# Modulation stores half a part later in SyncE's queue, output written tile by tile, and constant products ahead of the turns

## The chip, the cores and the metric

The kernel runs on one core of a Trainium2 chip. Its engines work side by side, each through a queue of its own in order: TensorE (PE) multiplies, VectorE (DVE) and ScalarE (ACT) do elementwise work, GpSimd (POOL) computes small roots and starts the gathers, and SyncE (SP) starts transfers. An engine whose next instruction waits on a semaphore holds everything that is queued behind it. The metric is the device time of one execution in microseconds (us); less is better.

## The reference

Two networks are computed one after the other on the same x (256 tokens of 1024), all in f32. The first is two layers of a hybrid mixer (retention and a state-space scan) and a SwiGLU. The second is two layers with modulated norms, latent attention with a context of 256 tokens, Fourier and pooling branches, and an expert layer that gathers 128 rows of 2 x 1024 numbers for each token. The parts that the change touches:

```python
def _modulation(cvec, w_mod, b_mod):
    m = jax.nn.silu(cvec) @ w_mod + b_mod          # 1024 -> 6 x 1024, for c and for c_ctx, in each of 2 layers
    return jnp.split(m[:, None, :], 6, axis=-1)

def _modulate(x, g, shift, scale):
    return _rmsnorm(x, g) * (1 + scale) + shift

def _rmsnorm(x, g):
    xf = x.astype(jnp.float32)
    y = xf * lax.rsqrt(jnp.mean(xf * xf, axis=-1, keepdims=True) + EPS)
    return (y * g.astype(jnp.float32)).astype(x.dtype)
...
# the last steps: x + m5 * peer(modulate(x, ...)), then the final norm, which is the output
```

## The kernel before

**How it is laid out.** A class `Plan` writes one list of work items by hand (`put(kind, ...)`). Each engine's program then goes through that list once and issues what it has to do for each kind, so every engine's order is the list's order. Two streams are merged into the list by paces: the x stream (first network, then the second network on x) and the context stream (the modulation rows, then the context's first layer). The 256 tokens are two tiles (`tt`) of 128 rows. PSUM is used as eight banks that are handed out in rings (`take()`); `u.full` and `u.free` are the semaphores of a bank.

**The modulation** (`modulation`, lines 571 and after) runs in the context stream beside the first network's first layer. It has six parts (2 layers of 3), each 2048 columns wide, each summed over k = 0 to 7. For each k, GpSimd loads one 1 MB piece of `wmod` (`mod_weights`, L2202), and TensorE multiplies it (`mod`, L1281). After k = 7 VectorE adds the bias with four small instructions (`mod_add`, L1702), and SyncE stores the rows to DRAM (`mod_store`, L2254, four transfers that begin with a wait for that add). The rows are read back later by `mod_load` (L2264) and `load_row` (L2272).

**The weights of the first network** are loaded by the same SyncE queue (`weights`, L2227), 1 MB for each chunk of 256 columns, from a ring of three buffers: a load waits until TensorE is done with the chunk three before it. Three such loads are therefore the most that stand ready. A chunk is 16 products of 128x128 by 128x256 (L1089, two rows of the trace for each product).

**The norms ahead of turns.** In `norm_to_hT` and `modulate` ScalarE sums squares (L1968), VectorE scales the sum (L1499), GpSimd takes the root (L2196), the rows are scaled, and TensorE turns them by transposes (L1124, `row_turn` and `mod_turn`). `low_rank` has the same chain between a product and its turn. TensorE waits meanwhile.

**The expert layer** (`peer_x`) gathers 256 pieces of 1 MB (L2209). Buffers: 11 in layer 0, and 15 in layer 1, where four more come from the side arena (`spare`). For each piece VectorE forms a dot product (L1902), and after every four TensorE adds the second halves up (L1445). `add(tt)` (L1921, L1925) adds the tile's sum to X: tile 0 at step 140 of 256, tile 1 at the end.

**The end.** After both tiles are added, `final` loads the norm's gain row (L2288), sums the squares of both tiles (L1968), takes the root, scales both (L1682) and stores the whole output, 1 MB, with one transfer (L2290).

## Time and profile before

| | us |
|---|---|
| median of three runs | 4399.33 (4393.66 to 4401.11) |
| the profiled execution, its own time | 4395.78 |
| its span, first to last instruction | 4394.5 |
| TensorE busy | 3679.7 (84% of the span) |
| VectorE busy | 2364.5 (54%) |
| ScalarE busy | 599.5 (14%) |
| GpSimd busy | 1311.6 (30%) |
| mean granted TensorE clock | 0.921 of full speed |

Busy shares are means over stages with different limits. The timeline of SyncE's queue and of TensorE shows what each stage waits for; the views of waits add those up. In a view of windows, PEclk is the granted TensorE clock as a share of 2.4 GHz (0.50 is the lower level, 1.2 GHz), and the DMA share is the busy share of the 16 DMA engines.

### The profile page before, as it was taken

Reading aid. Unit: us, or ns where it says so; the run is one execution under the profiler, and the core shown is the slowest. Engines: PE = TensorE matmul, PEld = TensorE weight load, DVE = VectorE, ACT = ScalarE, POOL = GpSimd, SP = SyncE. Lnnn points to the kernel's source line nnn. Section 1 sums busy time; section 2 is a strip of 40 time slices with the busy share of each in tenths; the row PEclk is TensorE's granted clock in tenths of the full one; section 3 lists DMA queues with packets and bytes.
Section 4 is the critical chain, followed back from the end, with each engine's and each line's share of the span. In section 5 each row is a group of like instructions: output and inputs, shape, how many; then the busy total and the mean of one; then the engine's idle time right before and its main releaser. Section 6 shows DMA issues by size and latency. Waiting matters only on the chain. (4 is left out here: it accounts for less than half of the span.)

```text
span 4394.5 us, 40482 instructions
## 1 busy us (share of the span) xinstructions
PE 3679.7 (84%) x14400; PEld 2592.9 (59%) x14400; DVE 2364.5 (54%) x5571; ACT 599.5 (14%) x1567; POOL 1311.6 (30%) x1123
## 2 busy tenths in 40 slices
PE   7777899998898778999996898778776898877777
PEld 5555778887765667887854776333333687333332
DVE  3332111258667777767652114776774212877774
ACT  1112200110001111010001201111111221111111
POOL 1000000000574435766530002444442001444442
PEclk9888999999898888999997999988988999999999
DMA  8542233433898768999982246998997234999997
GB/s 309 211 178 109 96 145 148 158 125 125 324 407 338 258 228 304 399 408 380 381 319 88 96 147 270 421 410 335 419 421 306 104 115 184 396 421 421 421 421 312
DMA packets 209527, 1214.89 MB, mean 276 GB/s; under 512 B 23872, under 2 KB 25024, under 8 KB 97712
## 3 DMA queue, kind: packets, MB, share of 16 engines
q0 software_dynamic: 154368, 855.71, 48.8%
q1 hardware_dynamic: 54960, 356.60, 21.5%
q8 instruction: 117, 1.92, 0.2%
q14 instruction: 82, 0.67, 0.0%
HBM read 1211.07 MB, written 1.15 MB: 276 GB/s over the span
## 5 line engine op out<-in xcount | busy, mean ns | idle before, releaser
L1089 PE MATMUL bank<-big 128*128 128x256 f32 (+3 forms) x9848 | 2179.4, 382 | 142.5 <-DMA big<-in_w 78.6
L1089 PEld LDWEIGHTS bank<-big 128*128 128x128 f32 x9848 | 1857.8, 194 | 466.3 <-issue 148.0
L2209 POOL DMA_INDIRECT big<-in_pboth,big x1024 | 1246.6, 1217 | 1259.4 <-PE bank L1445 622.8
L1445 PE MATMUL bank<-big 128*128 128x512 f32 x2048 | 1000.5, 647 | 282.5 <-ACT big L2170 282.5
L1902 DVE CUSTOM_DVE_ANT_0 big<-big 128x1024 f32<-128x1024 f32 x768 | 923.1, 1223 | 308.5 <-DMA big<-in_pboth,big 300.2
L1445 PEld LDWEIGHTS bank<-big 128*128 128x128 f32 x2048 | 414.0, 207 | 866.1 <-issue 494.7
L2196 POOL TENSOR_TENSOR big<-big 128x2 f32<-128x2 f32 (+1 forms) x47 | 39.1, 835 | 1617.7 <-DVE big L1499 1617.3
L1913 DVE SCALAR_TENSOR_TENSOR big<-big 128x1024 f32<-128x1024 f32 x254 | 326.1, 1284 | 27.9 <-DMA big<-in_pboth,big 4.4
L1124 PE MATMUL bank<-big 128*128 128x128 f32 x572 | 105.7, 326 | 193.4 <-ACT big L1982 72.0
L1124 PEld LDWEIGHTS bank<-big 128*128 128x128 f32 x572 | 80.0, 170 | 217.3 <-issue 188.3
L2170 ACT ACTIVATE big<-big 128x128 f32<-128x128 f32 x512 | 164.3, 391 | 250.6 <-DVE big L1881 246.5
L1267 PE MATMUL bank<-big 128*128 128x512 f32 x352 | 152.1, 593 | 3.3 <-DVE big L1668 3.3
L1572 DVE SCALAR_TENSOR_TENSOR big<-big,bank 128x512 f32<-128x512 f32 x32 | 22.0, 687 | 209.3 <-ACT big L2008 198.9
L1556 DVE SCALAR_TENSOR_TENSOR big<-bank,big 128x255 f32<-128x255 f32 (+1 forms) x144 | 62.7, 477 | 129.8 <-ACT big L1996 128.1
L2160 ACT ACTIVATE big<-big 128x4 f32<-128x4 f32 x128 | 26.5, 207 | 767.8 <-DVE big L1877 767.8
L1267 PEld LDWEIGHTS bank<-big 128*128 128x128 f32 x352 | 66.4, 189 | 88.1 <-issue 83.3
L1758 DVE TENSOR_REDUCE big<-bank 128x1 f32<-128x512 f32 (+1 forms) x48 | 28.9, 603 | 161.5 <-PE bank L1346 160.6
L1780 DVE SCALAR_TENSOR_TENSOR big<-big,bank 128x512 f32<-128x512 f32 x36 | 24.8, 689 | 147.4 <-PE bank L1089 147.4
L1654 DVE SCALAR_TENSOR_TENSOR big<-big,bank 128x256 f32<-128x256 f32 x32 | 13.4, 420 | 138.9 <-PE bank L1089 128.5
L2202 POOL DMA_DIRECT2D big<-in_wmod x48 | 25.8, 542 | 198.7 <-PE bank L1281 198.7
L1968 ACT ACTIVATE big<-big 128x1024 f32<-128x1024 f32 x26 | 27.2, 1048 | 423.7 <-DVE big L1675 154.8
L1499 DVE TENSOR_SCALAR big<-big 128x2 f32<-128x2 f32 (+1 forms) x47 | 7.2, 161 | 123.2 <-ACT big L1968 116.9
(192 smaller groups left out, 2060.8 us busy)
## 6 DMA issues: line engine op xcount, KB each, us to landing
big<-in_w SPq DMA_DIRECT2D x104, 1024.0 KB
big<-in_wmod POOLq DMA_DIRECT2D x48, 1024.0 KB, 7.2
big<-in_wgu SPq DMA_DIRECT2D x44, 1024.0 KB
big<-in_wzg SPq DMA_DIRECT2D x36, 1024.0 KB, 4.8
big<-in_wro SPq DMA_DIRECT2D x32, 1024.0 KB
big<-in_wpq SPq DMA_DIRECT2D x24, 1024.0 KB, 4.8
big<-in_wd SPq DMA_DIRECT2D x22, 1024.0 KB
big<-in_pboth,big POOLq DMA_INDIRECT x1024, 14.9
```

The source lines that it names most:

```text
L1089: last = pe.matmul(o, a, b, start=(i == 0), stop=(i == n - 1))
L1124: last = pe.transpose(o[:, i, :], b, ident)
L1267: last = pe.matmul(u.ap, act[:, kk, tt * P:tt * P + P], wk[:, k, 512 * n:512 * n + 512], start=(kk == 0), stop=(kk == 21))
L1445: last = pe.matmul(u.ap, d.ap, row[:, 512 * i:512 * i + 512], start=(k == 0), stop=(k == 127))
L1556: i = v.scalar_tensor_tensor(c[:, m, s:256], o[:, m, 0:256 - s], conv["w"][m][:, 3 - s:4 - s], c[:, m, s:256], ALU.mult, ALU.add)
L1758: step(v.reduce_max(sm[:, c:c + 1], u.ap[:, 0:nk * P], AX.X))
L1902: v.tensor_tensor_reduce(row, row, h, 1.0, 0.0, ALU.mult, ALU.add, out).then_inc(done[0], 1)
L1913: v.scalar_tensor_tensor(at, s.ap, by, at, ALU.mult, ALU.add).then_inc(done[0], 1)
L1968: last = s.activation(dumps[tt], srcs[tt], ACT.Square, accum_out=r.sm[:, r.at + tt:r.at + tt + 1])
L2170: s.activation(d.ap, p.ident, ACT.Copy, scale=by).then_inc(diag[0], 1)
L2196: g.tensor_tensor(r.sm[:, 8 + r.at:8 + r.at + r.n], r.sm[:, 4 + r.at:4 + r.at + r.n], r.sm[:, 12:13].to_broadcast([P, r.n]), ALU.pow).then ...
L2209: g.indirect_dma_start(out=s.ap, out_offset=None, in_=table, in_offset=bass.IndirectOffsetOnAxis(ap=index, axis=0)).then_inc(s.full[0], 16)
```

## The change

Three things are changed.

1. **Stores.** `mod_store` of a part is kept back in a list (`late`) and put into the order just before the item `mod` with k = 3 of the next part. The last part's store stays where it was, after the loop.
2. **Output.** The final norm becomes one for each tile. Tile 0's statistics follow its `add(0)` at step 140, its scaling and its store (0.5 MB) are put at step 168; tile 1's follow `add(1)`. The gain row is loaded with the last mod row, at the start of the gather. It and a scratch row take the place of one of the four spare gather buffers (15 become 14). SyncE waits for both stores in a last item `finished`.
3. **Constant products.** TensorE gets products of the identity with a constant 128x256 tile, written into the bank that the turn is about to fill and then overwritten by it: 8 ahead of the wait for the root and 2 behind it in the four `norm_to_hT`; 12 and 7 in the four modulated norms of x; 8 ahead of the first turn in the four `low_rank` of x. That is 148 products.

```diff
+    def rstd_of(self, sm, at, mul, add):
+        key = "a" if sm is self.small else "b"
+        r = Rstd(sm, 1, at, mul, add, self.stat_end.get(key), self.tick("squares_done"), self.tick("var_done"),
+                 self.tick("rstd_done"))
+        self.stat_end[key] = r.var
+        return r
...
-                                   [side.get(2048) for _ in range(4)] if l else [])
+                                   [side.get(2048) for _ in range(3)] if l else [], side if l else None)
...
+                    if k == 3 and late:
+                        put("mod_store", **late.pop())
                     put("mod", w=w, u=u, cc=cc, k=k, ready=(self.sem("mod_c_done"), 1) if l + part + k == 0 else None,
                         done=done)
...
-                put("mod_store", dst=[rows[:, 2048 * part + 512 * j:2048 * part + 512 * j + 512] for j in range(4)],
-                    src=[s.ap[32 * j:32 * j + 2, :] for j in range(4)], ready=u.free, done=stored[turn])
+                late.append(dict(dst=[rows[:, 2048 * part + 512 * j:2048 * part + 512 * j + 512] for j in range(4)],
+                    src=[s.ap[32 * j:32 * j + 2, :] for j in range(4)], ready=u.free, done=stored[turn]))
+        put("mod_store", **late.pop())
...
+        if last:
+            fw, fw_ok, dump = last.get(1024), tick("d_final", 16), last.get(1024)
+            put("load_row", dst=fw, src=t["fnorm"][1].to_broadcast([P, 1024]), done=fw_ok, before=[ended["keys"]])
...
             if n == 128 + 12:
                 add(0)
+                if last:
+                    r = final_stats(0)
+            if last and n == 128 + 40:
+                final_rows(0, r)
...
         add(1)
+        if last:
+            final_rows(1, final_stats(1))
...
+    def keep_busy(u, n):
+        for _ in range(n):
+            pe.matmul(u.ap[:, 0:256], ident, p.masks, start=True, stop=True)
...
             if g == 0:
+                if r:
+                    keep_busy(u, 12)
+                    pe.wait_ge(*r.done)
+                    keep_busy(u, 7)
                 pe.wait_ge(*done)
...
+            if tt == 0:
+                keep_busy(v, warm)
             pe.wait_ge(*scaled[tt])
...
-    def final(fw, loaded, normed, stored, before, **_):
-        q.wait_ge(*before)
-        q.dma_start(fw, t["fnorm"][1].to_broadcast([P, 1024])).then_inc(loaded[0], 16)
+    def final(X, normed, dst, stored, **_):
         q.wait_ge(*normed)
-        q.dma_start(p.out.rearrange("a (t p) d -> p (a t) d", p=P), p.X).then_inc(stored[0], 16)
+        q.dma_start(dst, X).then_inc(stored[0], 16)
+
+    def finished(stored):
         q.wait_ge(*stored)
```

**Place one: SyncE's queue from the first store to the third.** `w1` are the first network's weight chunks, `mods` the stores (the first of a group of four is the one that waits). Before:

```order
13 L2227 DMA big<-in_w1 128x2048 x4
14 L2254 DMA mods<-big 2x512 x4
15 L2227 DMA big<-in_bmod 128x512
16 L2227 DMA big<-in_w1 128x2048 x3
17 L2254 DMA mods<-big 2x512 x4
18 L2227 DMA big<-in_bmod 128x512
19 L2227 DMA big<-in_w1 128x2048 x2
20 L2254 DMA mods<-big 2x512 x4
```

The same place in the changed kernel (its lines are numbered some 40 higher):

```order
13 L2269 DMA big<-in_w1 128x2048 x4
14 L2269 DMA big<-in_bmod 128x512
15 L2269 DMA big<-in_w1 128x2048
16 L2296 DMA mods<-big 2x512 x4
17 L2269 DMA big<-in_w1 128x2048 x2
18 L2269 DMA big<-in_bmod 128x512
19 L2269 DMA big<-in_w1 128x2048
20 L2296 DMA mods<-big 2x512 x4
21 L2269 DMA big<-in_w1 128x2048
22 L2269 DMA big<-in_bmod 128x512
23 L2269 DMA big<-in_w1 128x2048 x2
24 L2296 DMA mods<-big 2x512 x4
```

The first, second, fourth and fifth store stand behind one more weight chunk, the third behind two, and the sixth behind as many as before.

**Place two: TensorE at the kernel's start**, the turns ahead of the first chunk. Before:

```order
0 L1124 MATMUL bank<-big 128x128 [waits barrier_Pool_Activation_PE_DVE_SP_release,rows_scaled,consts_done,d_consts]
1 L1124 MATMUL bank<-big 128x128 x7
2 L1124 MATMUL bank<-big 128x128 [waits rows_scaled,free4]
3 L1124 MATMUL bank<-big 128x128 x3
```

And now:

```order
0 L1162 MATMUL bank<-big 128x256 [waits barrier_Pool_Activation_PE_DVE_SP_release,consts_done,d_consts]
1 L1162 MATMUL bank<-big 128x256 x7
2 L1162 MATMUL bank<-big 128x256 [waits rstd_done]
3 L1162 MATMUL bank<-big 128x256
4 L1152 MATMUL bank<-big 128x128 [waits rows_scaled]
5 L1152 MATMUL bank<-big 128x128 x7
6 L1152 MATMUL bank<-big 128x128 [waits rows_scaled,free4]
```

The products stand ahead of the turn; the turn's own wait (`rows_scaled`) is kept.

**Place three: GpSimd's queue at the end**, the gathers of layer 1 and the root of the final norm. Before:

```order
49 L2196 TENSOR_TENSOR big<-big 128x1 x2
50 L2196 TENSOR_TENSOR big<-big 128x2 x2
51 L2196 TENSOR_TENSOR big<-big 128x1 x2
52 L2209 DMA big<-in_pboth,big 128x2048 x256
53 L2196 TENSOR_TENSOR big<-big 128x2
```

And now:

```order
51 L2238 TENSOR_TENSOR big<-big 128x1 x2
52 L2251 DMA big<-in_pboth,big 128x2048 x150
53 L2238 TENSOR_TENSOR big<-big 128x1
54 L2251 DMA big<-in_pboth,big 128x2048 x106
55 L2238 TENSOR_TENSOR big<-big 128x1
```

Tile 0's root, which waits for its statistics, now stands between the gathers 150 and 151.

## Rows read from the trace of the kernel before

**Rows 1.** Waits of SyncE's queue: total us, times, longest.
```profile
SPq L2254 <- DVE big L1702: 265.2, 6, 58.8
```

**Rows 2.** Waits of TensorE from 0 to 520 us, same columns.
```profile
PE bank L1089 <- DMA big<-in_w: 74.6, 6, 21.8
```

**Rows 3.** Timeline of SyncE's queue: start, us, instructions (L2254 stores, L2227 loads).
```profile
95.99 1.19 SPq L2254 DMA_DIRECT2D mods<-big  x4
...
97.63 1.38 SPq L2227 DMA_DIRECT2D big<-in_w  x3
142.84 1.14 SPq L2254 DMA_DIRECT2D mods<-big  x4
...
185.14 1.14 SPq L2254 DMA_DIRECT2D mods<-big  x4
...
246.88 1.27 SPq L2254 DMA_DIRECT2D mods<-big  x4
...
248.59 1.45 SPq L2227 DMA_DIRECT2D big<-in_w  x3
```

**Rows 4.** Timeline of GpSimd: five modulation weights asked for at once.
```profile
244.88 2.65 POOL L2202 DMA_DIRECT2D big<-in_wmod  x5
```

**Rows 5.** Timeline of TensorE, chunks of the first network; in brackets idle before, releaser.
```profile
106.06 9.08 PE L1089 MATMUL bank<-big 128*128 128x256 f32 x32 [7.56 <-DMA big<-in_w]
...
119.24 7.10 PE L1089 MATMUL bank<-big 128*128 128x256 f32 x32
...
149.53 9.53 PE L1089 MATMUL bank<-big 128*128 128x256 f32 x32 [6.14 <-DMA big<-in_w]
...
163.71 7.20 PE L1089 MATMUL bank<-big 128*128 128x256 f32 x32
...
197.93 9.23 PE L1089 MATMUL bank<-big 128*128 128x256 f32 x32 [17.14 <-DMA big<-in_w]
...
261.72 9.75 PE L1089 MATMUL bank<-big 128*128 128x256 f32 x32 [21.81 <-DMA big<-in_w]
...
280.12 7.20 PE L1089 MATMUL bank<-big 128*128 128x256 f32 x32
...
312.13 10.14 PE L1089 MATMUL bank<-big 128*128 128x256 f32 x32 [3.37 <-DMA big<-in_w]
...
358.64 9.09 PE L1089 MATMUL bank<-big 128*128 128x256 f32 x32 [18.58 <-DMA big<-in_w]
```

**Rows 6.** Timeline of GpSimd's root, then of TensorE at a modulated norm and low-rank turns.
```profile
2323.39 0.55 POOL L2196 TENSOR_TENSOR big<-big 128x1 f32<-128x1 f32 x1 [4.06 <-DVE big L1499]
...
2333.44 1.94 PE L1124 MATMUL bank<-big 128*128 128x128 f32 x8 [18.05 <-DVE big L1715]
...
2352.03 0.56 PE L1124 MATMUL bank<-big 128*128 128x128 f32 x2 [2.26 <-ACT big L2081]
2352.51 5.31 PE L1089 MATMUL bank<-big 128*32 128x256 f32 x16
...
2374.57 0.78 PE L1124 MATMUL bank<-big 128*128 128x128 f32 x4 [2.62 <-ACT big L2081]
```

**Rows 7.** Windows: PE, PEld, DVE, ACT, POOL busy, PEclk, DMA share, GB/s.
```profile
3666.00:3670.00 4.00, 0.00 (x0) 0.00 (x0) 0.00 (x0) 0.00 (x0) 0.02 (x1) 0.58 0.98 253
```

**Rows 8.** Timeline of the end, all engines.
```profile
4384.39 1.06 ACT L1968 ACTIVATE big<-big 128x1024 f32<-128x1024 f32 x1 [8.41 <-DVE big L1925]
...
4387.90 2.48 DVE L1682 SCALAR_TENSOR_TENSOR big<-big 128x1024 f32<-128x1024 f32 x2 [1.05 <-DMA big<-in_fnorm]
4390.41 0.40 SPq L2290 DMA_DIRECT2D out<-big  x1
```

**Rows 9.** Windows over layer 1's gather, columns as in rows 7.
```profile
3780.00:4360.00 580.00, 453.97 (x940) 187.59 (x939) 441.12 (x1244) 88.97 (x306) 265.44 (x231) 0.93 1.01 421
```

**Rows 10.** Gathers, issue to landing: layer 1, 3780 to 4362.
```profile
DMA to landing us min/median/max: 16.9/24.0/25.6
```

**Rows 11.** The same for layer 0, 2720 to 3290.
```profile
DMA to landing us min/median/max: 10.8/12.7/16.4
```

More of the change, by code:

```diff
@@ L214, in order @@
         self.streams(self.x_stream(ar), self.context_stream(), PACES[0])
-        ar.at = self.xmark
-        fw = ar.get(1024)
-        dump = ar.get(2048, (2, 1024))
-        r = self.rstd(self.small, 2, 1.0 / 1024, EPS)
-        self.put("final", fw=fw, dump=dump, r=r, loaded=self.tick("d_final", 16), normed=self.tick("out_ready"),
-                 stored=self.tick("d_out", 16), ready=self.x_ok, before=self.x_ok)
+        self.put("finished", stored=(self.sem("d_out"), self.counts["d_out"]))
     def streams(self, a, b, pace):
@@ L639, in modulate @@
             us = [banks.take() for _ in range(2)]
-            put("mod_turn", h=h[:, tt, :], us=us, dst=hT[:, :, tt * P:(tt + 1) * P], done=done[tt])
+            put("mod_turn", h=h[:, tt, :], us=us, dst=hT[:, :, tt * P:(tt + 1) * P], done=done[tt],
+                r=None if vec or tt else rs[0])
             yield 2
@@ L648, in low_rank @@
         self.put("low_rank", ws=ws, wt=wt, hT=hT, ready=ready, n=n, u=u, tmp=tmp, dst=dst, gcols=gcols, r=r, parts=parts,
+                 warm=8 if sm is self.small else 0,
                  scaled=[self.tick("lowrank_rows"), u.free])
@@ L976, in peer_c, with peer_x @@
         self.c_ok, self.b_free = end, [end]
-    def peer_x(self, banks, sm, start, size, l, X, side, spare):
+    def peer_x(self, banks, sm, start, size, l, X, side, spare, last):
         put, tick, t = self.put, self.tick, self.t
@@ L1052, in add, with final_stats, final_rows @@
             put("peer_part", us=by_pe[tt], m5=m5, m5_ok=m5_ok, tmp=h2[:, tt, :], X=X[:, tt, :], done=self.x_ok)
+        def final_stats(tt):
+            r = self.rstd_of(sm, tt, 1.0 / 1024, EPS)
+            put("row_stats", src=X[:, tt, :], dump=dump, r=r, ready=self.x_ok)
+            return r
+        def final_rows(tt, r):
+            put("final", X=X[:, tt, :], by=sm[:, 8 + tt:9 + tt], fw=fw, r=r, loaded=fw_ok, normed=tick("out_ready"),
+                dst=self.out[0, tt * P:(tt + 1) * P, :], stored=tick("d_out", 16))
         for n, (tt, k) in enumerate(steps):
@@ L1287, in mod_turn, with low_rank @@
             if g == 0:
+                if r:
+                    keep_busy(u, 12)
+                    pe.wait_ge(*r.done)
+                    keep_busy(u, 7)
                 pe.wait_ge(*done)
             turn(u, [h[:, (4 * g + i) * P:(4 * g + i + 1) * P] for i in range(4)]).then_inc(u.full[0], 1)
-    def low_rank(ws, wt, hT, ready, n, u, tmp, parts, scaled, **_):
+    def low_rank(ws, wt, hT, ready, n, u, tmp, parts, scaled, warm, **_):
         opened(u)
@@ L2212, in gpsimd_program @@
     kinds = dict(consts=consts, mod_weights=mod_weights, row_stats=root, group_gate=root, score_v=root, full_norm=root,
-                 low_rank=root, final=root, fetch=fetch)
+                 low_rank=root, fetch=fetch)
     for kind, args in p.items:
```

31 lines of the change are left out of this document (17 added, 14 removed).

## The prediction

> **What bounds the kernel now.** I read the waits of SyncE's queue first, since the change moves instructions there. Six waits of the modulation stores for VectorE's bias add hold the queue for 265.2 us, up to 58.8 at a time [rows 1]. That alone costs nothing; what counts is who waits for the weight loads behind them. TensorE's waits up to 520 us answer it: 74.6 us in six waits for `in_w` [rows 2]. The two timelines side by side show the pairing: the first store ends its wait at 95.99, the next weight load is issued at 97.63, and TensorE's chunk at 106.06 starts after 7.56 us of idling; each of the six stalls (7.56, 6.14, 17.14, 21.81, 3.37, 18.58) stands behind one store in this way [rows 3, 5]. Up to three loads are in hand when a store begins to wait, about 22 us of TensorE work without the modulation's products between, and the wait is longer than that. In this stretch TensorE has work whenever weights are there, so a stall removed moves everything behind it forward. Elsewhere TensorE waits for chains of small steps (18.05 us at a modulated norm [rows 6]) or, in the gathers, the DMA engines are the limit: share 1.01 and 421 GB/s over 580 us of layer 1's gather [rows 9].
>
> **Stores: what goes.** A chunk is 32 rows of TensorE and takes 7.20 us at full clock, 7.10 or 7.20 where nothing held it up. Behind the six stalls it takes 9.08, 9.53, 9.23, 9.75, 10.14 and 9.09 [rows 5], since the clock fell while TensorE stood still: 1.88, 2.33, 2.03, 2.55, 2.94 and 1.89 us more. The first five stalls sum to 56.02 us, their slow chunks to 11.73, together 67.75. The sixth (18.58 + 1.89) I leave in whole: its store is not moved in the order.
>
> **Stores: what is late next.** Each moved store now waits for the same add, but one more weight load (two for the third) is issued ahead of it. Whether TensorE runs through depends on the first load issued behind the store: issued just after the add, it must land before its chunk is due. In the trace such loads are issued and land thus: 97.63 for the chunk at 106.06, 8.4 us; 248.59 for the one at 261.72, 13.1 us, with five 1 MB modulation weights asked for at 244.88 just ahead of it [rows 3 to 5]; the other stalled chunks lie between 5.1 and 11.2. I shift the old times by what has been saved before them: 9.44 after the first stall, 17.91 after the second, 37.08 after the third, 61.44 after the fourth.
> - First store: issued at 97.2 to 97.6; its chunk, which ran at 119.24, is due at 109.8, 12.2 later. Landing takes 5.1 to 13.1. No stall (0.5 us at the worst).
> - Second: the add is done at 142.84 - 9.44 = 133.4, the load out at 134.9, the chunk of 163.71 due at 145.8. That leaves 10.9 us; 2.2 missing at the worst landing.
> - Third: done at 185.14 - 17.91 = 167.2, due at about 191. No stall.
> - Fourth: done at 246.88 - 37.08 = 209.8, load out at 211.0, the chunk of 280.12 due at 218.7. That leaves 7.7, and the five modulation weights are asked for at 207.8 here too, so I take the 13.1 us landing: a stall of 5.4, and 2.2 for the slow clock after it. 7.6 us stay.
> - Fifth: its stall was 3.37 and one chunk of 7.20 more is now in hand. No stall.
>
> The gain is 67.75 - 7.6 = 60 us. If landings of 13.1 come everywhere, 0.5 and 2.2 are added with a slow chunk behind each (2 x about 2.2), and with some more on the fourth it is 52.8; if none comes, 67.8. VectorE's adds are small and no other step of the stretch is late by tens of us, so that I let the later stages move forward as a whole. The rows are stored up to 25 us later, but their first reader stands behind the sixth store, whose place in the queue is as before: nothing.
>
> **Output by tiles.** At the end there are now two squares of 1.06 us (ScalarE), a root, a wait of 1.05 us for the gain row, two scalings in 2.48 us and a store issued at 4390.41 [rows 8], which lands some 4.1 us later, at the end of the span. Changed, only tile 1 is left: one square less (about 1.1), no wait for the gain row (0.2 of its 1.05 counted beside the root that stays), one scaling less (1.24): 2.5 us earlier. Half the bytes of the store save 0 to 1.2 us (0.5 MB at 421 GB/s [rows 9]); near 0 if its time is mostly latency.
> The Trainium skill ("DMA: Bandwidth & Descriptors", Anatomy of one DMA) puts some 2.0 us of any transfer down to a fixed part, mostly its completion; of the 4.1 us here the bytes of 1 MB would be 2.5 at the rate of rows 9, which leaves 1.6, so that row and rule roughly agree and half of it would be the 1.2 above.
> Against it: tile 0's store of 0.5 MB goes out in the middle of a gather that has all the bandwidth [rows 9], 1.2 us; the gain row's load there, 0 to 1.2. One spare buffer less: layer 1's pieces take 24.0 us from issue to landing [rows 10], layer 0's with eleven buffers 12.7 [rows 11]; a piece moves in 1.049 MB / 421 GB/s = 2.49 us, so that is 9.6 and 5.1 pieces in flight. Five keep the engines full in layer 0 at the same rate, so one of ten less costs nothing, 2.5 us as a bound. GpSimd's root for tile 0 now holds up the gathers behind it, and VectorE the dot products behind its scaling, by 2 to 5 us; the 9.6 pieces in flight (24 us) cover both. Without that cover it would be those 5 us. Sum: -1, from -2.5 to +2.5.
>
> **Constant products.** 148 products, each 128x256 and so 7.20 / 16 = 0.45 us at full clock, 0.90 at the lower one. They cost nothing where they end before the turn's input is ready, and give what the turn and the products behind it gain by clock. At the four modulated norms the root ends at 2323.94 and the turn starts at 2333.44 [rows 6], 9.5 us later (8.5 to 10.6 in the four); the 7 products behind the root take 3.2 us, or 6.3 at the lower clock. They end before, so cost 0; gain 0 to 6.6 over four, since TensorE stands still again for 4 us and more between. That a pause of this size drops the clock the trace shows: at 3666 to 3670 it was 0.58, with TensorE idle and little else running [rows 7]. I take -1. At the four `norm_to_hT` the two products behind the root take 0.9 of the 1.3 us that the scaling needs: cost up to 0.7 and gain up to 3, I take -1. The four `low_rank` are different, as the 8 products are 3.60 us and the wait before the turn was 2.26 or 2.62 [rows 6]: the turn comes 1.34 and 0.98 later, 4.6 in all. Against it, the 16 products behind took 5.31 where 3.60 is full clock [rows 6], 1.71 lost; the four places lose 5.8 by their products and 0.9 by their turns. I take -1.5 net of -2.1. Sum of the three -3.5, from -13 to +6.
>
> **The sum.** 60 + 1 + 3.5 = 64.5 off the profiled execution's 4395.78 gives 4331.3. The median of the runs lies 3.6 above that execution (4399.33), so 4334.8; the last 2 us I leave out as half of what separates the fastest run shown (4393.66) from the profiled one. I say 4333, the point from which the chances are counted. Some 0.2% (9 us) is about what a measurement of this kernel can tell from no change.
>
> **Rivals.**
> (a) *Landings keep stalls.* TensorE runs faster through the stretch, so chunk weights and modulation weights (24 or more MB in some 290 us) come more crowded. If the load behind the fourth store lands no sooner than before against its due time, 24.4 us stay and not 7.6; with the second's 8.5 as well the gain is 60 - 16.8 - 8.5 = 35. Time 4350 to 4358. For it: the five weights at 244.88 [rows 4]; against: 5 to 9 us landings for the most. 14%.
> (b) *The order changes and nothing else.* If the stalls were made by the DMA engines and not by the queue, the loads would land as late when issued earlier: gain under 9, some 4391. Against it: the loads are issued 1.6 us after the store's wait ends, every time [rows 3]; the wait is the queue's. 4%.
> (c) *Slower: one buffer less in layer 1's gather, with the root in GpSimd's queue.* If pieces then came at 2.74 us in place of 2.49, 256 of them lose 64 us, all that the rest gains; from 2.78 (75 us) the kernel is slower by more than 0.2%. Against it: layer 0 runs at the same rate with eleven [rows 11]. Time 4408 or more. 2%.
> (d) *The products only cost.* If the clock has fallen again by the time of the turn, the modulated norms and `norm_to_hT` give nothing and `low_rank` costs its 4.6: 8.1 us poorer than my sum, 4341. For it: the pause of at least 4 us after the 7 products, and rows 7. 8%.
> On (d) the Trainium skill ("TensorE: Matmul & The Clock Gate", Part 1) says that the lower rate is the default, that sustained work lifts it and that an idle pause puts it back; by that the products of the modulated norms, with a pause behind them, buy nothing, which is the time of (d) for that term.
>
> **How the numbers follow.** My forecast 72%, (a) 14, (b) 4, (c) 2, (d) 8. The range begins at the best of all terms, 67.8 + 2.5 + 6.5 off (half of the products' best, since all of it needs four places each at their bound): 4318 to 4320, I say 4318. It ends at 4358, with (a) in it, since otherwise more than 2 in 10 would be left out. Faster by over 0.2%: 72 + 14 + 8 = 94; within 0.2% (b) 4; slower (c) 2.
>
> **What would show it.** In the changed kernel's trace TensorE's waits for `in_w` up to 520 us should be 19 to 27 us in all, with one of about 18.6 behind the last store. The stretch should end 58 to 66 us earlier, so that the turn at 2333.44 comes at about 2272. Layer 1's gather should still show 421 GB/s over its length, and the last VectorE scaling one tile of 1.24 us. At the modulated norms TensorE should show 12 + 7 products and a pause of 3 to 7 us before the turn; a granted clock at 1 there would speak for the upper end of their gain. I am wrong if waits for `in_w` of 30 us or more stay, if a new wait of VectorE or SyncE takes their place, or if a piece of the gather takes over 2.55 us.

## The result: 4323 us, 1.7% faster, and where the profile after shows it

| | before | changed |
|---|---|---|
| median, us (4 runs each) | 4397.86 (4393.66 to 4401.11) | 4323.14 (4321.52 to 4324.37) |
| ratio, 95% interval | | 0.983 (0.9813 to 0.9847) |
| span of the profiled execution | 4394.5 | 4322.9 |
| mean granted TensorE clock | 0.921 | 0.936 |

The change takes 74.7 us off by the medians and 71.6 by the spans; 66 were forecast. The waits answer [rows 1] and [rows 2] first. SyncE's queue in the changed kernel (total us, times, longest):

```profile
SPq L2296 <- DVE big L1745: 181.2, 6, 40.1
```

and TensorE up to 520 us:

```profile
PE bank L1117 <- DMA big<-in_w: 20.0, 2, 18.3
```

The queue still waits 181 us for the bias adds (265.2 before), six times as before. Much less is spent waiting for the queue: 20.0 us in two waits, where there were 74.6 in six. The timeline of TensorE shows both, against [rows 5]:

```profile
222.67 7.17 PE L1117 MATMUL bank<-big 128*128 128x256 f32 x32 [1.75 <-DMA big<-in_w]
...
293.97 9.40 PE L1117 MATMUL bank<-big 128*128 128x256 f32 x32 [18.28 <-DMA big<-in_w]
```

The stall behind the fourth store is 1.75 us and no longer 21.81, and its chunk runs at full speed (7.17). The one behind the sixth store, whose place is unchanged, is as it was (18.28, and a slow chunk of 9.40; before 18.58 and 9.09).

Laid side by side, each VectorE instruction of the changed kernel has its twin in the kernel before. How much earlier it starts, as medians over stretches (read from the two traces; times of the kernel before):

| stretch, us | earlier by | what lies ahead of it |
|---|---|---|
| 120 to 160 | 9.0 | first store |
| 160 to 200 | 17.7 | second |
| 200 to 240 | 38.1 | third |
| 272 to 278 | 60.9 | fourth |
| 320 to 360 | 64.4 | fifth |
| 480 to 1960 | 64.0 to 64.2, 62.2 around 1400 | first network |
| 2400 to 2600 | 67.5 to 69.2 | modulated norm and low_rank, layer 0 |
| 2760 to 3390 | 67.1 to 67.6 | gather of layer 0 |
| 3450 to 3790 | 70.2, then 71.8 | norms and low_rank, layer 1 |
| 3830 to 4150 | 68.8 | start of layer 1's gather |
| 4170 to 4386 | 67.6 | store of tile 0 |
| end of the span | 71.6 | the last norm and store |

This ledger holds the three parts apart: 64 are won in the stretch of the stores, some 8 more by 3790 where only the products differ, the gather gives 4.2 back, and the end wins 4.0.

### The profile page after: what moved, and what is told of

It reads as the page before. It is cut to its first block and busy times, and to the rows that moved or that the text cites. A ratio compares the mean times of both kernels' runs of the same rounds, so it can differ in the third digit from the quotient of the medians.

```text
span 4322.9 us, 41067 instructions
## 1 busy us (share of the span) xinstructions
PE 3729.6 (86%) x14696; PEld 2641.6 (61%) x14696; DVE 2365.0 (55%) x5572; ACT 600.2 (14%) x1567; POOL 1314.0 (30%) x1124
## 5 line engine op out<-in xcount | busy, mean ns | idle before, releaser
L1117 PE MATMUL bank<-big 128*128 128x256 f32 (+3 forms) x9848 | 2157.3, 380 | 89.3 <-DMA big<-in_w 23.9
L1117 PEld LDWEIGHTS bank<-big 128*128 128x128 f32 x9848 | 1845.9, 193 | 402.1 <-issue 86.8
L1488 PEld LDWEIGHTS bank<-big 128*128 128x128 f32 x2048 | 415.1, 207 | 869.9 <-issue 496.4
L2238 POOL TENSOR_TENSOR big<-big 128x1 f32<-128x1 f32 (+1 forms) x48 | 40.2, 840 | 1602.9 <-DVE big L1542 1602.8
L1152 PEld LDWEIGHTS bank<-big 128*128 128x128 f32 x572 | 78.3, 166 | 117.4 <-issue 68.1
L1304 PEld LDWEIGHTS bank<-big 128*128 128x128 f32 x352 | 66.5, 189 | 87.7 <-issue 83.2
L1162 PE MATMUL bank<-big 128*128 128x256 f32 x296 | 73.8, 408 | 31.3 <-POOL big L2238 20.0
L1162 PEld LDWEIGHTS bank<-big 128*128 128x128 f32 x296 | 59.9, 205 | 43.3 <-POOL big L2238 21.6
```

The source lines that it names most:

```text
L1117: last = pe.matmul(o, a, b, start=(i == 0), stop=(i == n - 1))
L1152: last = pe.transpose(o[:, i, :], b, ident)
L1162: pe.matmul(u.ap[:, 0:256], ident, p.masks, start=True, stop=True)
L1304: last = pe.matmul(u.ap, act[:, kk, tt * P:tt * P + P], wk[:, k, 512 * n:512 * n + 512], start=(kk == 0), stop=(kk == 21))
L1488: last = pe.matmul(u.ap, d.ap, row[:, 512 * i:512 * i + 512], start=(k == 0), stop=(k == 127))
L2238: g.tensor_tensor(r.sm[:, 8 + r.at:8 + r.at + r.n], r.sm[:, 4 + r.at:4 + r.at + r.n], r.sm[:, 12:13].to_broadcast([P, r.n]), ALU.pow).then ...
```

## Experiments

Medians in us. "Below before" is the median of the kernel before, taken beside the run, less the run's.

| run | built on | median | ratio to before (95%) | below before | span |
|---|---|---|---|---|---|
| the change | before | 4323.14 | 0.983 (0.9813 to 0.9847) | 74.7 | 4322.9 |
| e1 stores only | before | 4338.70 | 0.986 (0.9842 to 0.9877) | 61.9 | 4337.8 |
| e2 output only | before | 4401.05 | 1.0001 (0.999 to 1.0011) | -0.4 | 4402.2 |
| e3 products only | before | 4390.13 | 0.9976 (0.9966 to 0.9986) | 10.5 | 4388.9 |
| e4 stores at k = 1 | before | 4367.75 | 0.9923 (0.9906 to 0.994) | 32.9 | 4365.1 |
| e5 14 buffers | before | 4402.45 | 1.0005 (0.9995 to 1.0015) | -2.4 | 4404.4 |
| e6 no low_rank products | changed | 4331.20 | 0.984 (0.9826 to 0.9853) | 68.8 | 4336.3 |
| e7 last store later | changed | 4312.79 | 0.9804 (0.9787 to 0.9822) | 87.2 | 4310.8 |
| e8 no mod_turn products | changed | 4328.61 | 0.9838 (0.9825 to 0.9852) | 71.4 | 4328.3 |
| e9 the same, 12 more elsewhere | changed | 4328.97 | 0.9836 (0.982 to 0.9852) | 72.2 | 4327.6 |
| e10 last store later, 16 buffers | changed | 4307.38 | 0.9791 (0.9772 to 0.981) | 93.8 | 4300.0 |
| e11 low_rank with 5 products | changed | 4322.41 | 0.9827 (0.981 to 0.9845) | 78.8 | 4319.9 |
| e12 e10 and e11 together | changed | 4303.99 | 0.9775 (0.9761 to 0.9789) | 100.4 | 4293.3 |

The medians of the kernel before were 4397.9 (the change), 4400.6 (e1 to e4), 4400.0 (e5 to e8), 4401.2 (e9 to e11) and 4404.4 (e12). They wander by some us, so two runs from different rows of this list are best compared by the column "below before". The intervals of e6, e8, e9 and e11 overlap that of the change for the most part: the times alone do not show that these four differ from it, and what is said of their parts rests on the traces, one for each kernel.

### The three parts alone

**Stores.** The edit is the hunk on `late` of the change, and nothing else.

> The kernel before with the store part of the change alone. Theory of the queue: five of the six waits of TensorE for in_w up to 520 us go, with the slow chunk behind each; 20 us of waits stay, 18 of them at the sixth store, and from 400 us on every VectorE instruction comes 64 us earlier than before and stays so. Time about 64 below the kernel before, 4334. Rival, a transfer bound: if loads were late because of the DMA engines, the gain would be under 9 us. Second rival: part of what the whole change gained in this stretch came from its constant products, then this run gains under 60.

Measured: 4338.7, 61.9 us below the kernel before.

```profile
PE bank L1092 <- DMA big<-in_w: 21.9, 2, 19.0
```

Two waits, as in the whole change (here 2.90 and 18.98 us). VectorE is 59.0 us ahead at 400 to 480 us, and between 56.4 and 60.0 in the later stages that I compared. This run lost 1.9 us to the kernel before ahead of the first store, where nothing is changed: TensorE's first 128 rows took 30.12 us in it and 28.00 in the profiled execution before. The first ones are 0.43 us apart in e1 until 26.3 us, when its granted clock rises to 1.00, and 0.22 from there on; in the profiled execution before it rises at 21.2, ahead of these rows. So the stores are worth 61 (59.0 + 1.9) to 64, and the theory of the queue stands. The rival of a transfer bound falls; the second, that the whole change won part of this through its products, is open for 3 us. They are the fourth stall with its slow chunk, 4.6 us here and 1.75 in the whole change.

**Output.** The changed kernel with `mod_store` put at once, `r=None` for all turns and `warm=0`.

> The kernel before with the output part alone (final norm by tiles, 14 gather buffers in layer 1 and not 15, gain row loaded early). Nothing moves up to the gather of layer 1. There the changed kernel's trace lost 3.1 us at its start and 1.2 at tile 0's store, and won 1.3 + 2.7 behind its end. If these belong to this part, VectorE's dot products run 3.1 us late from the 20th piece on, 4.3 from tile 0's store on, and the span is within 0.5 us of before. Rival: the loss at the start came from the shifted phase of the earlier stages, and this part alone gains 2 to 4 us.

Measured: no change, 4401.05 against 4400.63. The span is 7.7 us above that of the profiled execution before, and not within 0.5 as expected: by the traces 2.2 of it arise before anything is changed, and 4.9 in a wait at the start of the gather that the profiled execution before did not have (below). To see what the part itself does, VectorE's dot products of layer 1 (one for each gathered piece) are a clock of the gather. From the 25th to the 129th, from there to the last, and from the last to the end of the span:

| run | buffers | output | 25th to 129th | 129th to 256th | to the end |
|---|---|---|---|---|---|
| before, e1, e3, e4 | 15 | whole | 255.4, 256.1, 255.8, 255.8 | 321.6, 321.7, 321.7, 321.7 | 22.0, 22.3, 22.3, 23.9 |
| changed, e2 | 14 | by tiles | 258.4, 258.9 | 322.9, 322.9 | 18.1, 18.1 |
| e5 | 14 | whole | 259.3 | 321.6 | 22.1 |
| e10 | 16 | by tiles | 254.9 | 322.9 | 18.1 |

Output by tiles costs about 3 us early in the gather and 1.2 us in its second half, and wins 4.0 behind it (2.2 in e7, e9 and e12, where the last stretch took 19.8). Why that stretch takes 19.8 in some kernels and 18.1 in others is not known. The 4.0 can be read off the end of the changed kernel, against [rows 8]:

```profile
4316.80 1.06 ACT L2013 ACTIVATE big<-big 128x1024 f32<-128x1024 f32 x1 [8.42 <-DVE big L1968]
...
4318.96 1.28 DVE L1986 SCALAR_TENSOR_TENSOR big<-big 128x1024 f32<-128x1024 f32 x1 [0.76 <-POOL big L2238]
4320.28 0.34 SPq L2330 DMA_DIRECT2D out<-big  x1
```

From the square's start to the store's issue it is 3.5 us and was 6.0: 2.5 less, as forecast. From the issue to the end of the span 2.6, and it was 4.1: half the bytes save 1.5, above my bound of 1.2. The Trainium skill ("DMA: Bandwidth & Descriptors", Anatomy of one DMA) gives some 2.0 us as the part of a transfer that does not depend on its size, in a section on transfers that GpSimd starts, while SyncE starts this one. An estimate from that page is 2.0 and 1.25 for the bytes at 421 GB/s, 3.25; measured are 2.6, so the fixed part is smaller here, 1.4 (and 1.6 for the 1 MB).

**Fourteen buffers.** One number in the kernel before, to price the buffer by itself:

```diff
-                                   [side.get(2048) for _ in range(4)] if l else [])
+                                   [side.get(2048) for _ in range(3)] if l else [])
```

> The kernel before with 14 gather buffers in layer 1 in place of 15, nothing else. In the kernel before, VectorE's dot products of layer 1 take 255.5 us from the 25th to the 129th piece; 14 buffers with output by tiles took 258.4 and 258.9. Theory: one piece less is in hand when the gather becomes saturated, which costs one piece's 2.5 us once, whatever comes later: 258 here and about 403 from the 129th piece to the last but no 1.2 us more; time 2.5 us above before. Rival of the prediction (c): the rate falls, then the rest of the gather is longer too. Second rival: the gain row's load made the loss, then this run shows 255.5.

Measured: 259.3 from the 25th to the 129th and 321.6 from there on, as in the kernel before (the 403 of the expectation is a slip). The buffer costs some 3 us once (2.9 by the means of all kernels with 15 and with 14), early, and nothing later: the gather still moves 421 GB/s. In time this is 2.4 us, within the noise (interval -2 to 7). This also settles rival (c) of the prediction, since a lower rate would have lengthened the second half. The gain row's load is not the cause, as this kernel has none there. The 1.2 us of the second half come only with tile 0's store, and 0.5 MB at 421 GB/s are 1.25.

**Products.** The hunks on `keep_busy` alone, on the kernel before.

> The kernel before with the 148 constant products alone. Theory: they give 6 to 8 us, since the changed kernel's lead grows from 64.0 to 71.8 us between 1640 and 3700 us, where only they differ. Rival (d) of the prediction: they give nothing at the norms and cost 4.6 at low_rank, the lead came from the phase of other stages, and this kernel is 0 to 5 us slower than before.

Measured: 4390.13, 10.5 us faster by the medians (interval 6 to 15) and 5.6 by the spans. They do give something, against rival (d), and more than the 3.5 forecast. Together e1, e2 and e3 sum to 61.9 - 0.4 + 10.5 = 72 us, beside 74.7 of the whole change: within the noise the parts do not disturb each other.

### What a store's place is worth

```diff
-                    if k == 3 and late:
+                    if k == 1 and late:
```

on e1. SyncE's queue then has:

```order
15 L2257 DMA mods<-big 2x512 x4
16 L2230 DMA big<-in_w 128x2048 x3
17 L2230 DMA big<-in_bmod 128x512
18 L2257 DMA mods<-big 2x512 x4
19 L2230 DMA big<-in_w 128x2048 x2
20 L2230 DMA big<-in_bmod 128x512
21 L2230 DMA big<-in_w 128x2048
22 L2257 DMA mods<-big 2x512 x4
```

The first two stores have the same chunks ahead of them as before, the third one more.

> The kernel before with each store put ahead of k = 1 of the next part and not k = 3. In SyncE's queue the third and fourth store then stand behind one more weight chunk, the first, second, fifth and sixth behind as many as before. Theory of the queue: only the third and fourth stall go (17.14 + 2.03 and 21.81 + 2.55), the others stay at 7.6, 6.1, 3.4 and 18.6 us; gain 36 to 43.5, time about 4358. Rival: what counts is that the store comes later in time, not the chunk ahead of it, then all five shrink alike.

Measured: 4367.75, 32.9 below before, where 36 to 43.5 were expected. In the trace VectorE goes from 2.1 us late ahead of the first store to 35.6 early at 360 us, 37.7 in all; from 1100 us on 31 to 33 are left. The stalls, one for each store:

```profile
106.89 9.41 PE L1092 MATMUL bank<-big 128*128 128x256 f32 x32 [6.30 <-DMA big<-in_w]
...
150.49 9.79 PE L1092 MATMUL bank<-big 128*128 128x256 f32 x32 [5.93 <-DMA big<-in_w]
...
197.73 10.06 PE L1092 MATMUL bank<-big 128*128 128x256 f32 x32 [5.38 <-DMA big<-in_w]
...
247.72 8.85 PE L1092 MATMUL bank<-big 128*128 128x256 f32 x32 [2.82 <-DMA big<-in_w]
...
278.98 7.17 PE L1092 MATMUL bank<-big 128*128 128x256 f32 x32 [1.30 <-DMA big<-in_w]
...
323.40 8.69 PE L1092 MATMUL bank<-big 128*128 128x256 f32 x32 [19.17 <-DMA big<-in_w]
```

The first, second and sixth stalls are nearly as before (6.30, 5.93 and 19.17 where there were 7.56, 6.14 and 18.58), the third and fourth fell from 17.14 and 21.81 to 5.38 and 2.82. So what counts is how many chunks stand ahead of the store, and not how late it comes. It also shows that one chunk of 7.2 us is not always enough, which k = 3 hides: there the third store has two. The fifth stall (3.37 before, 1.30 here) shrank with no chunk more; that is left unexplained.

**The last store.** On the changed kernel:

```diff
+        yield 14
         put("mod_store", **late.pop())
```

The sixth store, and the whole context stream behind it, then comes two chunks of x later.

> The changed kernel with the sixth store put behind two more weight chunks, and all of the context stream behind it as much later. Theory: the sixth stall is made like the others and goes: TensorE's waits for in_w fall from 20.0 us to under 3, the stretch ends 18 + 2 us earlier, time about 4303. Rival: the read back of the rows and the later context stream give it back, as a new wait in SyncE's queue or as context work that is left over when the gather begins; then the gain is under 10 us.

Measured: 4312.8 (runs from 4303.65 to 4320.78), 12.5 more below the kernel before than the change is (the two intervals still overlap a little), and 12.1 by the spans, where 20 were expected. TensorE up to 520 us:

```profile
PE bank L1153 <- DVE big L1759: 5.0, 2, 4.1
...
PE bank L1118 <- DMA big<-in_w: 3.7, 2, 2.9
```

The stall is gone as the theory has it (3.7 us of waits for `in_w` in all), and VectorE is 22 us ahead of the changed kernel behind the stretch. But a new wait of 5.0 us for the context's modulated rows (L1759) stands there, 16 us are left at 1100, 14 at the gather of layer 1, and 12 at the end. Theory and rival are both true in part: of the 20 us expected some 8 are not there at the end. That the later context stream takes them is argued from that one wait; no run isolates it.

### What the constant products do

**low_rank.** As a measure I take, for each of the four turns, the wait ahead of the turn and the time of the 80 rows of TensorE that follow, and sum them. Without products ahead of them (before, e1, e2, e4, e5, e6): 124.0, 122.9, 119.4, 124.8, 124.8, 124.1, mean 123.3. With 8 (changed, e3, e7, e8, e9, e10): 120.0, 120.0, 118.8, 120.1, 120.1, 119.7, mean 119.8. They give 3.5 us by the means, where I took 1.5; e2 reached 119.4 without them.

```diff
-                 warm=8 if sm is self.small else 0,
+                 warm=0,
```

> The changed kernel without the 8 products ahead of each low_rank turn. By the prediction they delay four turns by 4.6 us in all and regain up to 6.7 us in the turns and products behind: this kernel is 0 to 3 us slower than the changed one. By the rival (the clock has fallen anyway, or the products behind do not follow) it is 2 to 4.6 us faster.

Measured: 4331.2 (4323.1 to 4337.6), 8 above the changed kernel's median and 5.9 less below the kernel before; the expectation was 0 to 3. The first of the four places, without products:

```profile
2287.78 0.56 PE L1152 MATMUL bank<-big 128*128 128x128 f32 x2 [2.26 <-ACT big L2126]
2288.26 5.33 PE L1117 MATMUL bank<-big 128*32 128x256 f32 x16
```

and in the changed kernel:

```profile
2283.56 3.62 PE L1162 MATMUL bank<-big 128*128 128x256 f32 x16
2287.02 0.38 PE L1152 MATMUL bank<-big 128*128 128x128 f32 x2
2287.33 3.65 PE L1117 MATMUL bank<-big 128*32 128x256 f32 x16
```

16 rows behind the turn take 3.65 and not 5.33: the clock is kept over a wait of 3 us if TensorE works through it. The profiled execution of e6, its slowest, ended 13.4 us behind the changed kernel's: 4.1 of them at the four places and 5.4 in a wait at the gather, below. With five products:

```diff
-                 warm=8 if sm is self.small else 0,
+                 warm=5 if sm is self.small else 0,
```

> The changed kernel with 5 and not 8 products ahead of a low_rank turn. They end 2.25 us after the product, where the wait for the turn's rows ended 2.26 or 2.62 after it. Theory: the turns come as early as without products (gaps of 2.26 and 2.63, not 3.29) and the turns and products behind stay as fast as with 8 (23.6, 31.5, 23.2 and 28.6 us for the 80 rows behind the four turns, without products 25.3, 32.9, 24.6, 31.5): 3.4 us faster than the changed kernel, and 7 faster than without. Rival: 5 are too few to keep the clock, then the rows behind are as slow as without any.

```profile
2283.72 2.32 PE L1162 MATMUL bank<-big 128*128 128x256 f32 x10
2286.06 0.65 PE L1152 MATMUL bank<-big 128*128 128x128 f32 x2
2286.64 3.65 PE L1117 MATMUL bank<-big 128*32 128x256 f32 x16
```

Measured: the products behind are as fast (3.65) and the four places take 115.0 us, 5.0 less than with 8. The median is the changed kernel's (4322.4), the distance from the kernel before 4.1 more. The trace was 10.9 us ahead of the changed kernel's at 3480 us, of which only the 5.0 can be read off the four places, and 3.8 at 3700, behind the wait at the gather of layer 1.

**The modulated norms.** `r=None` in `mod_turn`.

> The changed kernel without the 12 + 7 products of the four modulated norms. By the prediction's sum they give 1 us, and by its rival (d) nothing, since TensorE pauses 4 to 7 us between them and the turn: same time as the changed kernel within 1.5 us. The other end of the term is 6.6: then the turns and the products behind them run slower here, at 1.94 us for the first 8 rows of a turn against less in the changed kernel, and the kernel is 4 to 7 us slower.

Measured: 4328.6, 5.5 above the changed kernel's median (3.3 less below the kernel before), which looks like the upper end. The traces say otherwise: just ahead of the gather, at 3620 to 3640 us, the run is 0.7 us behind the changed kernel, and the 5 us come at the gather. At the first norm in the changed kernel:

```profile
2258.75 6.16 PE L1162 MATMUL bank<-big 128*128 128x256 f32 x14 [3.23 <-POOL big L2238]
2268.62 1.97 PE L1152 MATMUL bank<-big 128*128 128x128 f32 x8 [3.72 <-DVE big L1758]
```

Seven products take 6.16 us, 0.88 each, the price at the lower clock: it had fallen by then, after 3.23 us of waiting between the two groups. The granted clock shows the rest (columns as in rows 7; the products, the pause behind them, the turn):

```profile
2258.70:2265.00 6.30, 6.16 (x14) 4.55 (x14) 0.46 (x2) 0.22 (x2) 0.55 (x1) 0.53 0.61 196
2265.00:2268.60 3.60, 0.00 (x0) 0.00 (x0) 3.46 (x4) 0.00 (x0) 0.00 (x0) 0.92 0.00 0
2268.60:2271.00 2.40, 1.97 (x8) 1.57 (x8) 2.37 (x2) 0.96 (x2) 0.00 (x0) 0.50 0.00 0
```

The products lift the clock, but only as they end, and it is back at 0.50 when the turn begins. The turn takes 1.97, without products 1.94. At this norm they buy nothing, as rival (d) has it. The rule cited with that rival, from the Trainium skill ("TensorE: Matmul & The Clock Gate", Part 1), agrees with these rows.

It is not so everywhere. Of the seven kernels that have the products, the 80 rows of TensorE from the second norm's turn on take 18.8 to 18.9 us in four (e3, e7, e10, e12) and 20.6 to 21.2 in three; without products 20.8 to 21.0. From the fourth norm's on they take 18.8 to 19.1 in three (the changed kernel, e3, e10) and 20.6 to 22.1 in four; without 20.4 to 21.6. In e3 the turn of the second norm still runs at a granted clock of 0.50 behind a pause of 6.04 us, but the rows behind it at 1.00 (0.87 in the kernel before). So the products can bring 2 us forward at these two places, in half of the cases; as means over the seven kernels with and the seven without, 1.1 and 0.6 us. What decides it is open.

**A wait that depends on something else.** In e8, 15 us after the first gather of layer 1:

```profile
3641.82 7.20 PE L1116 MATMUL bank<-big 128*128 128x256 f32 x32
3648.86 1.05 PE L1477 MATMUL bank<-big 128*128 128x128 f32 x8
3652.82 8.88 PE L1116 MATMUL bank<-big 128*128 128x256 f32 x32 [2.91 <-ACT big L2189]
```

and at the same place in the changed kernel:

```profile
3641.15 7.20 PE L1117 MATMUL bank<-big 128*128 128x256 f32 x32
3648.19 1.05 PE L1478 MATMUL bank<-big 128*128 128x128 f32 x8
3649.09 7.20 PE L1117 MATMUL bank<-big 128*128 128x256 f32 x32
```

TensorE waits 2.9 us for ScalarE's copy out of a full bank, and the slow chunk behind adds 1.7. But ScalarE is not what is late. Its copy waits for the semaphore that TensorE raises at the end of the chunk, and so does SyncE's next load of `in_wpq`. In e8 both start together, at 3652.18 and 3652.12:

```profile
3641.12 11.33 SPq L2268 DMA_DIRECT2D big<-in_wpq  x2
3652.18 0.59 ACT L2189 COPY big<-bank 128x512 f32<-128x512 f32 x1 [9.52 <-remote]
```

The profile models the chunk's end at 3649.02, and the semaphore moves at 3652.10, 3.1 us later; in the changed kernel it moves within 0.02 us of the modelled end. So it is TensorE's own chunk that ends late, though its rows as the profile models them do not show it. Over the fourteen kernels this lateness is 0.01 to 0.4 us in five (before, changed, e3, e7, e10), 1.0 to 1.1 in three (e4, e9, e12) and 2.4 to 4.0 in six (e1, e2, e5, e6, e8, e11), and these six are the ones where TensorE then waits (2.2 to 3.8 us). What it costs can be read too: from the first gather to the 25th dot product the eight kernels without the wait take 87.0 to 88.1 us, five of the six with it 91.8 to 92.7, and e1, with the shortest wait, 89.4.

The two kinds of kernel go in part with the moment at which one 16 KB packet of TensorE's instructions starts: 5.0 to 5.3 us after the first gather in the changed kernel, e3, e7, e9, e10 and e12, none of which waits; 8.6 to 10.3 (or 20.0, e6) in the others, of which before and e4 did not wait. e9 tested it, by putting 12 products (48 instructions) at a place where TensorE idles anyway:

```diff
                 put("row_turn", src=hn[:, tt, :], dst=hT[:, :, tt * P:(tt + 1) * P], us=us, ready=hs[tt], scale=scale,
-                    r=None if tt else rs[0])
+                    r=None if tt else rs[0], more=12 if scale is second[0] else 0)
...
-                    keep_busy(u, 8)
+                    keep_busy(u, 8 + more)
```

> The kernel of the run without mod_turn products, with 12 more products ahead of the first turn of the second norm (1044 us), where TensorE waits 16 us anyway. In five of ten kernels profiled so far TensorE waits 2.2 to 3.7 us for a copy of ScalarE (L2189 there) 15 us after the first gather of layer 1 is issued, and its next chunk takes 8.9 us and not 7.2. In those the 16 KB instruction packet of that moment starts 9.2 to 10.3 us after the first gather, or none comes near; in the three kernels with all 148 products, which never waited, it starts at 5.0. Theory of the phase: the wait depends on where TensorE's count of instructions puts that fetch. 12 products are 48 instructions, some 5 us earlier: the packet comes at about 4, the wait goes, and the time is 5 us below the run without them (4328.6), though no product at any modulated norm has come back. Rival: the wait hangs on the products of the norm itself; then it is still there and the time is as without.

Measured: the packet starts at 5.0 and the wait is gone, as the theory has it, but the time is 4328.97, as without the 12. The profiled execution lost 3 us at the last norm and the first chunks behind it instead. So the wait costs some 5 us in an execution that has it, but that moving the packet saves time is not shown. The link with the packet is a coincidence in fourteen traces, one for each kernel, with two exceptions; whether other executions of the same kernel wait is not known. Why TensorE's chunk ends late is open.

### Better than both

**e10** has e7's later store, puts the gain row and the scratch row into the context's state (free in layer 1) and gets a 16th buffer from the context's keys.

```diff
-                                   [side.get(2048) for _ in range(3)] if l else [], side if l else None)
+                                   [side.get(2048) for _ in range(4)] + [self.whole_kc] if l else [], self.C if l else None)
...
-            fw, fw_ok, dump = last.get(1024), tick("d_final", 16), last.get(1024)
+            fw, fw_ok, dump = last[:, 0, :], tick("d_final", 16), last[:, 1, :]
```

> The changed kernel with the sixth store two chunks later and 16 gather buffers in layer 1: the gain row and the scratch row lie in the context's state, which is free by then, so that the fourth spare buffer is back, and the keys of the context layer, free too, make one more. Theory: with each buffer one more piece is in hand when the gather becomes saturated, 2.9 us once (255.8 us with 15 and 258.7 with 14 from the 25th to the 129th dot product): some 253 us here; time 6 us below the kernel with the last store later (4312.8), 4307. Rival: with 15 the limit is already something else (when TensorE and VectorE are done with the first pieces), then 255.8 and 4310.

Measured: 4307.4, 5.4 below e7's median (6.6 by the distance from the kernel before, 10.8 by the spans). The stretch from the 25th to the 129th dot product is 254.9 us, 3.6 less than e7's 258.5; the rest of the difference is elsewhere and not explained. The 15th buffer is worth 2.9; the 16th some 0.7 (254.9 here and 255.3 in e12, beside 255.4 to 256.1 with 15). The rival is right on the 16th.

**e12** adds five products at low_rank and the 12 that this saves at the second norm of the first network.

> The kernel with the last store later and 16 buffers (4307.4), with 5 products ahead of each low_rank turn and the 12 that this saves put ahead of the first turn of the second norm, so that TensorE's count of instructions ahead of layer 1's gather is as before. Theory: the four low_rank places take 5.0 us less (gap and 80 rows behind: 25.4, 33.3, 25.1 and 31.3 us, with 8 products 26.9, 34.8, 26.5 and 31.8), the instruction packet comes 5 us after the first gather and TensorE does not wait there; span about 4295, time 4302. Rival: the wait of 2 to 4 us at the gather comes whatever the packet does, as the run without mod_turn products and 12 more gained nothing in time; then the dot products start 4 to 5 us later and 4307 stays.

Measured: 4304.0 (4294.7 to 4311.2), ratio to the kernel before 0.9775. The four low_rank places take 114.6 us, the packet comes at 5.1, there is no wait at the gather, and the span is 4293.3, 6.7 below e10. By the medians it is 3.4, and 6.6 by the distance from the kernel before, less than the spread of its five runs; that e12 beats e10 is shown by the traces alone. Both beat the changed kernel: their intervals (up to 0.981 and 0.9789) end below that of the change (from 0.9813), and by the distance from the kernel before they are 19 and 26 us further down.

## Why the prediction was right, step by step

**Right.** The bound and the mechanism: six waits of SyncE's queue, six stalls of TensorE behind them, five of which go, but for 1.75 us, with one more chunk ahead. Shifting the old times by what had been saved was accurate to under 1 us: the second to fourth adds were forecast for 133.4, 167.2 and 209.8, and the stores behind them stand at 133.85, 167.11 and 210.44; the five modulation weights were forecast for 207.8 and asked for at 208.45; 20.0 us of waits for `in_w` lie in the stated 19 to 27. The turn of 2333.44 came 64.8 us earlier, at 2268.62 and not at about 2272; 58 to 66 were stated. Rival (a) (14%) fell: no large stall stayed. Rival (b) (4%) fell by e4, where nearly all of the gain is at the two stalls whose store has another place among the chunks. Rival (c) (2%) fell by e5. The last 2 us of the sum were a slip: half of 4395.78 - 4393.66 is 1.1, which would give 4333.7 and changes nothing.

**A size that was off: the fourth stall.** I took the worst landing of the trace, 13.1 us, and so 5.4 of stall and 2.2 of slow chunk. The load was issued at 211.78 and its chunk started at 222.67, 10.9 later, 2.2 sooner than I took; and the chunk was due at 220.92 and not 218.7. The stall was 1.75, and the chunk behind it was not slow. By the ledger 64 us were won in this stretch, 4 more than forecast, and this stall, 5.9 us smaller than forecast, is the reason. In e1 it was 2.90 with a slow chunk of 8.86 behind it, 4.6 in all, and the stores alone gave 61.

**Output.** The sum (1 forecast, 0 measured) hides two terms that were off and cancel: a buffer less cost 2.9 and not 0, and the half store saved 1.5 where 0 to 1.2 stood. The step that failed is "five keep the engines full, so one of ten less costs nothing". It is true for the rate: 421 GB/s with 14, 15 and 16 buffers. My reading is that before the gather is saturated each buffer is a piece asked for while the engines have room, a head start worth one piece's 2.5 us, once. That the loss comes once and early is shown; the head start is argued, and the 16th buffer, worth 0.7, does not follow it. My bound of 2.5 nearly had the 2.9.

**Products.** 3.5 forecast, 10.5 measured by medians (6 to 15) and 5.6 by the spans: the size was off. Of this low_rank is 3.5 (1.5 forecast) and the modulated norms 0.7 by e8, or 1.7 as the mean of their second and fourth place (1 forecast). The start of the kernel is some 2 us ahead, where I took 1 for all four `norm_to_hT`. VectorE at 60 to 120 us stands from 0.7 us behind the kernel before to 3.1 ahead of it in the nine kernels with products there, mean 0.8 ahead, and 0 to 2.2 behind in the five without, mean 1.5 behind. The reason can be read: TensorE's first 128 rows take 28.00 us in all nine, and without products 29.6 to 30.3 in e1, e2, e4 and e5; only the profiled execution before had 28.00 as well. So the row that I reckoned from was the lucky one. The rest, some 4 us, I put down to how often the wait at the gather comes; it came in none of the four profiled kernels with just the change's 148 products (changed, e3, e7, e10), and in three of the five without any (e1, e2, e5, but not before and e4). This last piece is inferred from the traces; no run isolates it in time. No row of the kernel before could have told it: that execution did not wait there. Rival (d) was right at the first modulated norm and wrong at low_rank: there TensorE has no pause between products and turn.

The forecast gain of 66 us was thus 8 short: 4 of it in the stores (by the ledger), and 2 by the spans or 7 by the medians in the products; 1 was lost in the output.

## What to carry to other kernels

- A wait in a queue that is shared with loads costs what the loads behind it come late for. Count the pieces of work that stand ready ahead of it, in us, against the length of the wait; one place in the order took 20 us out of the fourth stall and the chunk behind it (e4). Do it for each wait: the last one was left as it stood, and was worth 12 more.
- Products that fill a wait keep the clock surely where they reach up to its end, and should end before the data is ready: at four waits of 2.3 to 2.6 us five of them gave 8 us, eight 3.5. Those with a pause of 3.7 us or more behind them gave nothing or, at two of four places and in half of the kernels, some 2 us.
- When a kernel changes by a few us, look at whether a wait far from the edit came or went before believing a price. e8 cost 5.5 us by the median and under 1 ahead of the gather.
- The engine that a wait is put down to need not be the late one. Look at what else waits for the same semaphore: SyncE's load beside ScalarE's copy showed that TensorE's own chunk ended late.

## What the runs showed that I had not expected

- The changed kernel's trace holds 119 instruction packets of 16 KB for 30499 instructions of TensorE, one for some 256. The moment at which one starts, against the first gathers, goes in part with a wait of 2 to 4 us (six kernels of fourteen), and an edit that changes TensorE's instruction count moves it: 9.2 us after the first gather in e8, 5.0 with 48 instructions more in e9.
- TensorE's semaphore at the end of a chunk moved up to 4.0 us after the end that the profile models (e11), with nothing to be seen in the rows of the chunk.
- A stop of TensorE of 1.75 us did not slow the chunk behind it (7.17); one of 2.90 in e1 at the same place did (8.86).
- The kernel ended 2.6 us after the issue of a store of 0.5 MB, and 4.1 after that of 1 MB.
